# Weight tiles interleaved in pairs and read with a step of 8 bytes, with rings at multiples of 256 bytes

## What is computed

```python
def _swiglu(u, w_in, w_out):          # w_in 1024 x 5632, w_out 2816 x 1024
    h = u @ w_in
    a, b = h[..., :D_FF], h[..., D_FF:]
    return (jax.nn.silu(a) * b) @ w_out
```

## Time and profile before

| | |
|---|---|
| median of three runs | 1888.41 us |
| profiled execution | 1891.49 us |
| its span, first to last instruction | 1889.7 us |
| TensorE matmuls busy | 1866.9 us (99%), 13,850 |
| TensorE weight loads busy | 1846.0 us (98%), 13,850 |
| VectorE / ScalarE / GpSimd busy | 66% / 46% / 17% |
| mean granted TensorE clock | 0.994 |
| HBM traffic | 123 GB/s over the span |

### The profile page before, as it was taken

The page is one execution under the profiler, slowest core; times in us unless marked ns, Lnnn a source line. Parts: engine busy times, 40 slices in busy tenths (PEclk is TensorE's granted clock), DMA queues, the critical chain, the costliest instruction groups (busy, mean ns, idle before and its releaser), DMA issues.

```text
span 1889.7 us, 34441 instructions
## 1 busy us (share of the span) xinstructions
PE 1866.9 (99%) x13850; PEld 1846.0 (98%) x13850; DVE 1249.8 (66%) x1999; ACT 867.4 (46%) x1518; POOL 329.7 (17%) x352
## 2 busy tenths in 40 slices
PE   8999999999999999999999999999999999999998
PEld 7999999998999999999999999999989999999998
DVE  7874487668874488678853885553446888448843
ACT  7652355346652355345532553232334665235532
POOL 2220122121210122132201221300010322012112
PEclk9999999999999999999999999999999999999999
DMA  8773576333773576347644763222113576357632
GB/s 213 158 159 93 128 167 146 107 91 95 158 157 95 127 168 150 103 107 170 142 127 106 171 136 101 84 101 67 57 45 104 115 176 149 102 122 167 129 95 79
DMA packets 116830, 234.71 MB, mean 124 GB/s; under 512 B 13184, under 2 KB 15248, under 8 KB 116672
## 3 DMA queue, kind: packets, MB, share of 16 engines
q1 hardware_dynamic: 77440, 160.59, 28.3%
q0 software_dynamic: 38208, 69.42, 22.2%
q10 hardware_dynamic: 1024, 2.49, 0.4%
HBM read 228.92 MB, written 3.53 MB: 123 GB/s over the span
## 4 chain that ended last, share of the span: by engine, by line
PE 91%; DVE 4%; ACT 2%; DMA 1%; issue 1%; DVEq 0%; ACTq 0%
PE ps L1859 48%; PE ps L1850 39%; DMA raw_y<-in_ffn_in 1%; DVE w_lo L1241 1%; DVE u L1295 1%; PE ps L2176 1%; PE ps L2242 0%; ACT w_hi L736 0%; PE ps L2179 0%; DMA x<-in_x 0%; PE ps L2041 0%; PE ps L2166 0%; PE ps L2151 0%; DVE rstd L1312 0%; ACT u L778 0%
## 5 line engine op out<-in xcount | busy, mean ns | idle before, releaser
L1859 PE MATMUL ps<-u,w_hi 128*128 128x288 f32 x4928 | 984.1, 295 | 11.8 <-DVE u L1295 4.6
L1859 PEld LDWEIGHTS ps<-u,w_hi 128*128 128x128 f32 x4928 | 790.5, 188 | 16.2 <-DVE w_lo L1241 8.5
L1859 PE MATMUL ps<-u,w_lo 128*128 128x288 f32 x2464 | 726.3, 295 | 0.0
L1859 PEld LDWEIGHTS ps<-u,w_lo 128*128 128x128 f32 x2464 | 462.5, 188 | 0.0
L1850 PE MATMUL ps<-h_lo,w_hi 128*128 128x256 f32 x1386 | 297.6, 296 | 0.0
L1850 PE MATMUL ps<-h_hi,w_hi 128*128 128x256 f32 x1386 | 297.5, 296 | 0.0
L1850 PE MATMUL ps<-h_hi,w_lo 128*128 128x256 f32 x1386 | 297.4, 297 | 0.0
L736 ACT ACTIVATE w_hi<-w_raw 128x768 fp32r<-128x768 f32 (+3 forms) x164 | 136.1, 836 | 322.2 <-PE ps L1850 247.3
L1241 DVE TENSOR_TENSOR w_lo<-w_raw,w_hi 128x768 fp32r<-128x768 f32 (+3 forms) x164 | 167.9, 1032 | 164.1 <-ACT w_hi L736 161.8
L1850 PEld LDWEIGHTS ps<-h_hi,w_lo 128*128 128x128 f32 x1386 | 234.0, 190 | 0.0
L1850 PEld LDWEIGHTS ps<-h_lo,w_hi 128*128 128x128 f32 x1386 | 234.0, 190 | 0.0
(11 more groups left out here) (268 smaller groups left out, 2136.3 us busy)
## 6 DMA issues: line engine op xcount, KB each, us to landing
raw_a<-in_ffn_in SPq DMA_DIRECT2D x132, 256.0 KB, 4.1
w_raw<-in_ffn_out SPq DMA_DIRECT2D x64, 384.0 KB, 3.2
raw_y<-in_ffn_in SPq DMA_DIRECT2D x88, 256.0 KB, 3.6
raw_x<-in_ffn_in SPq DMA_DIRECT2D x88, 256.0 KB, 2.7
raw_x<-in_ffn_in POOLq DMA_DIRECT2D x88, 256.0 KB, 6.4
raw_y<-in_ffn_in POOLq DMA_DIRECT2D x88, 256.0 KB, 4.9
raw_z<-in_ffn_in POOLq DMA_DIRECT2D x88, 256.0 KB, 5.0
w_raw<-in_ffn_out SPq DMA_DIRECT2D x64, 320.0 KB, 3.1
```

The costliest lines, as they stand in the source:

```text
L1859: mm = pe.matmul(dst, w, m, start=prod in ("M1", "M2", "M5") and kp == 0 and p == 0, stop=kp == KP - 1 and p == 2, skip_group_check=prod i ...
```

## The change

Two things. The weight rings begin at multiples of 256 bytes. And two neighbouring tiles of a unit are interleaved column by column: column 0 of the even tile, column 0 of the odd one, column 1 of the even one, and so on. The host arranges the weight arrays so, and TensorE's weight load takes every second column (a step of 2 elements, 8 bytes) over 1024 bytes. The eleventh inner tile of an output tile has no neighbour and stays as it was; so do the weights of the pool projections and of the gates.

```diff
+    align(256)
     w_hi, w_lo = sb("w_hi", [P, RING * ENTRY], F32R), sb("w_lo", [P, RING * ENTRY], F32R)
...
+            def tile_of(ring, u, kk):
+
+                if KEYS[u][2:3] == ("out",) and KEYS[u][4] == 1 and kk == OUT_UNIT[1] - 1:
+                    return ring[:, PLACE[u] + kk * P:PLACE[u] + (kk + 1) * P]
+                at = PLACE[u] + kk // 2 * 2 * P
+                return ring[:, at:at + 2 * P].rearrange("p (m two) -> p two m", two=2)[:, kk % 2]
+
             def passes(u, kk, m_h, m_l):
 
-                w = slice(PLACE[u] + kk * P, PLACE[u] + (kk + 1) * P)
-                return (w_hi[:, w], m_h), (w_hi[:, w], m_l), (w_lo[:, w], m_h)
+                w_h, w_l = tile_of(w_hi, u, kk), tile_of(w_lo, u, kk)
+                return (w_h, m_h), (w_h, m_l), (w_l, m_h)
...
+    def paired(w):
+
+        return w.reshape(w.shape[:-1] + (-1, 2, P)).swapaxes(-2, -1).reshape(w.shape)
+
     def ffn_in(w):
         w = np.asarray(w).reshape(2, KP, 2, P, 2, FT, P).transpose(0, 5, 4, 2, 3, 1, 6)
-        return w.reshape(2, FT, 4, P, ENTRY)
+        return paired(w.reshape(2, FT, 4, P, ENTRY))
 
     def ffn_out(w):
-        return np.asarray(w).reshape(2, FT, P, DT, P).transpose(0, 3, 2, 1, 4).reshape(2, DT, P, FT * P)
+        w = np.asarray(w).reshape(2, FT, P, DT, P).transpose(0, 3, 2, 1, 4).reshape(2, DT, P, 2, PAIRS * P)
+        even = (PAIRS - 1) * P
+        return np.concatenate([paired(w[..., :even]), w[..., even:]], -1).reshape(2, DT, P, FT * P)
 
     def square_w(w, n):
-        return np.asarray(w).reshape(DT, P, n, P).transpose(2, 1, 0, 3).reshape(n, P, DT * P)
+        return paired(np.asarray(w).reshape(DT, P, n, P).transpose(2, 1, 0, 3).reshape(n, P, DT * P))
```

## The result

The changed kernel takes 1903.05 us (three runs, 1902.89 to 1905.11) against 1888.41: the ratio is 1.0083, 95% interval [1.0059, 1.0106]. 1865 was forecast. Busy shares hardly moved, and the kernel is bound as before. The first lines are the page's busy line, the chain by line and three groups of weight loads (busy us, mean ns).

A forecast was written before the change was run, and what follows sets the result against it. TensorE's back-to-back matmuls were taken as the bound. Vanished load waits gave -23.5 us, repacking, rings and feeding nothing: 1868 from the profiled 1891.5, or 1865 against the 1888.4 median; 8-in-10 range 1755 to 1950.

The forecast's parts named there:

- The bound: Whole kernel: TensorE-bound, so time is the number of matmuls times their distance, 132.2 ns per product, 133.3 per block.
- The step of 8 bytes: 12,768 weight loads: at the stream's pace their mean waits vanish, 23.5 us less; ends nothing and 64 us.
- The ground for it: Stretch at 1.2 GHz and the norms' fp32 matmuls: excess 0 or 2 ns, taken as load and stream at equal pace.
- The rings: Weight rings moved to multiples of 256 bytes: the remainder against the streams taken not to matter, 0 us.
- The stepped load gets in the way: Rival: loads over 1,024 bytes meet the stream more, 5 ns for each of 12,768, 64 us, 1952; chance 0.25.
- Its other sign: In that slower rival, 528 blocks would lengthen by more than 924 products in proportion, 256-column windows being hit first.
- Whole excess gone: Rival: equal pace removes the matmuls' excess, 137 us less, 1751; chance 0.14, shared with any gain above 64 us.
- nothing changes: Rival: the excess belongs to the 4-byte stream at 2.4 GHz whatever the load does, 1888 within 0.3%; chance 0.22.
- half pace: Rival: stepped loads read half as fast and set 217 ns windows, 2960; chance 0.09, shared with other large losses.
- the direction that was called likeliest: Whole kernel: faster, chance 0.44 against 0.34 for slower; likeliest a small gain of 6 to 64 us, chance 0.30.

The follow-up runs named there:

- e7: Kernel before with the weight rings 64 bytes past a multiple of 256, small buffers packed to 32 bytes: 1881.4 us, ratio 0.9961.
- e8: Kernel before with h and um 192 bytes past a multiple of 256, rings left at 128: 1876.3 us, ratio 0.9932.
- b1_distances: Kernel before plus 21 stretches of 120 float32r matmuls behind its last one; at 288 columns, contiguous loads 131.7 or 133.3 ns, step of 8 133.3 ns.
- e4: Changed kernel with blocks cut into 288 and 288 columns instead of 256 and 320: 1893.8 us, ratio 1.0031 to the kernel before.
- e9: Kernel before with only the products' weights interleaved and read with a step of 8 bytes; blocks contiguous: 1898.2 us, ratio 1.0049.
- e1_align_only: Kernel before with the rings at multiples of 256 bytes, tiles and reads contiguous: 1883.2 us, ratio 0.9973.
- e2: Changed kernel without the ring alignment: step of 8 bytes, rings 128 past a multiple of 256: 1903.5 us, ratio 1.0082 to the kernel before.
- e3: The changed kernel measured once more, against the kernel before: 1902.2 us, ratio 1.0073.
- e5: Kernel before with rings at multiples of 256, contiguous reads and blocks of 288 and 288 columns: 1889.8 us, ratio 1.0011.
- e11: Kernel before with h and um at 0 past a multiple of 256, rings left at 128: 1878.7 us, ratio 0.9943.
- e6: Kernel before with blocks of 288 and 288 columns, rings where they were: 1879.0 us, ratio 0.9956.
- e10: Changed kernel's interleaved tiles and step of 8 bytes, with rings at 128, h and um at 192 past a multiple of 256: 1897.2 us, ratio 1.0049 to the kernel before.

## Why the prediction was wrong

**The bound, right.** The time is the number of matmuls times their distance; nearly all of the 13.6 us lie there, as do 4.7 of the 8 us that e7 gains and 11.5 of the 13 of e8, counted over the eight product and eight block stages alone.

**The step of 8 bytes, wrong: this is the step that failed.** "If the equal pace keeps load and stream apart, the mean waits go: 7,392 x 1 + 5,376 x 3 = 23.5 us less." The idea behind it was that a load running through as many bytes per ns as the stream would meet it less. The loads grew from 188 to 195 ns instead, and the distance by 1.1 ns in products and 1.0 in blocks. The price had a second fault: it took a ns of a load's wait for a ns of the window. In b1_distances loads of 188 ns stand beside windows of 131.7 and of 133.3.

Two things stand in its place. First, the stepped load is itself slower: its floor is 118.3 ns, not the 111.3 of a contiguous one, and windows of 256 columns grow by 2.4 ns beside it. Secondly, contiguous loads can settle into patterns of 130.0 to 132.2 ns with the right shift, and stepped loads into none below 133.3, except e4's blocks (132.5). The products of the kernel before sat in such a pattern (132.2, in one stage 131.1) and lost it; e9 shows that loss by itself, 9 us. What sets a pattern, and why the step takes it away, in terms of the memory, no run shows.

**The ground for it, misread.** The stretch at 1.2 GHz and the plain fp32 matmuls had no excess, or 2 ns, and equal pace as I read them, but also half the demand. I named the second reading in a rival and still took the first. The changed kernel has the equal pace at full demand, and the excess stayed at 13.3 ns. So equal pace isn't what freed those rows. For the first of them it isn't even shown. These are loads of the stretch at the 1.2 GHz level (ns min/median/max):

```profile
L1859 PEld LDWEIGHTS ps<-u,w_lo x4: 330/330/330, 11.9 to 14.0; 128*128 128x128 f32 x4
```

At the full clock a load lasts 188, of which 107 are reading. If the reading took 107 here too and only the other 81 doubled, a load would last 269. By this estimate the load read slower than the stream there. That half the demand freed them is left as the likely reason and was not tested by itself.

**The rings, wrong in the plain kernel.** They were costed at 0. Alone they gain 5 us, beside the step nothing that can be told. The remainder matters where loads are contiguous (131.7 against 133.3 ns in b1_distances), but most of the gain is in blocks and projections, whose remainders became unequal by the change.

**The rivals.** "The stepped load gets in the way" has the direction, and the loads of over 192 ns that it asked for. Its other sign failed: blocks were to grow by more than products in proportion, and grew by 0.75% against 0.84%, so the 256-column windows (8 ns over a floor of 110, not the 7 that were written) are not where most of the loss is; 8.2 of 13.9 us are in products of 288 columns. Its price was wrong too: 64 us for 5 ns in each window, 15 measured. It took the 5 ns of a load's own wait for 5 ns of the window. In b1 a load 5 to 8 ns longer changes the window by -1.0 (512 columns) to 2.4 ns (256), as long as the load is not the bound. "Whole excess gone", "nothing changes" and "half pace" fall; a half-pace load is real, but at a step of 16 bytes.

**The range and chances.** 1903 lay in 1755 to 1950 and in the 0.25 given to that rival, but the direction that was called likeliest was the other one. That it lay in the range is no merit of the mechanism: the range reached from the whole excess gone to 5 ns more for every load.

On the rules that were weighed: the Trainium skill ("Advanced Engine Details and Errata", SBUF Cachelines) asks for two hits on a 16-byte line for full pace. The cliff is there, since one hit (step of 16) takes 233.4 ns. The promise doesn't hold: two hits cost the load 6 to 7 ns, and a moving operand with two hits 257.8 instead of 133.3. Of the other rule of the Trainium skill, that weight loads take nothing from the running matmul ("TensorE: Matmul & The Clock Gate", step 1 of Part 2), the trace shows the opposite in effect: moving only the weights by 32 to 224 bytes changes the distance by up to 4 ns. No run shows by which way they meet.

## What to carry to other kernels

In this kernel, bound by back-to-back float32r matmuls of some 288 columns, each has 12 to 13 ns of excess, of which 1 to 3 can be had by choosing where weights and streams begin relative to each other (steps of 32 bytes matter), a line or two per buffer; 0.7% of the time was the most that came of it. Measure such layouts as stretches of the real order behind the kernel's last matmul, a line each, then in the whole kernel, since a stage may hold a better or a worse pattern. Prefer contiguous weight tiles: every stepped kernel was slower than its contiguous counterpart, though one kind of stage (blocks of 288 + 288) was 0.8 ns faster with the step. A step of 16 doubles the load.

## What was not expected of the hardware

- One stage of 528 blocks holds 130.0 or 133.3 ns to its end, with the same code and addresses (68.64 and 70.42 us in e1_align_only). What chooses is open; in the stretches of blocks a start shifted by one matmul of 130 columns changed nothing, while one of products took 131.2 and 132.3 ns in two kernels.
- A stream of 288 columns read with a step of 8 bytes takes 30.93 / 120 = 257.8 ns beside a contiguous load, nearly twice 133.3, while a weight load with the same step loses 7 ns. The granted clock was 0.50 in its first 5 us and 1.00 behind them, and the distance was the same within 2 ns.
- The granted clock can fall to the 1.2 GHz level in the middle of the kernel, in one profiled execution and not in another. These are windows in the same part of the mLSTM, of the kernel before and of e1_align_only (the third number from the end is the clock):

```profile
1300.00:1304.00 4.00, 4.00 (x17) 3.72 (x17) 1.67 (x2) 2.10 (x3) 0.00 (x0) 0.50 0.20 68
```

```profile
1292.00:1296.00 4.00, 4.00 (x29) 3.68 (x29) 1.98 (x2) 2.79 (x4) 0.00 (x0) 1.00 0.00 0
```

In front of these windows the engine ran blocks in groups of six with waits between them, in both kernels alike. The next 48 blocks take 8.01 us in the first and 6.44 in the second. The profiles of before, after, e2, e3, e5, e7, e9 and e11 have such a fall, and take 276.1 to 280.3 us from the last long stage before the mLSTM's projections to the first behind it; those of e1, e4, e6, e8 and e10 have none and take 272.3 to 275.7. So a difference of some 3 us between two profiled executions can be the clock's and not the layout's, and 6.0 of the 10.6 us between the profiles of e1 and of the kernel before lie in this part, the projections' own gain among them.
